# A two-layer decoder trunk on one Trainium2 core: the whole panels of the mixing sub-layers become split panels, and 14 of their low parts are formed by an adding DMA

## The reference

```python
h = modulate(x, 0)
x = x + 0.5 * gate(0) * swiglu(h, ffn_wg[l, 0], ffn_wu[l, 0], ffn_wd[l, 0])

h = modulate(x, 1)
z = h @ w_in[l]
q, k, v, u, gates = jnp.split(z, SPLITS, axis=-1)
q = apply_rope(...); k = apply_rope(...)
...  # 3 dilated windows x 4 heads, merged by a softmax over their denominators
y_attn = o.astype(x.dtype).reshape(b, s, ATTN_OUT_W) @ attn_wo[l]
y_conv = conv_module(u, conv_w[l], conv_b[l], conv_ln_g[l], conv_ln_b[l], conv_wo[l])
y = jax.nn.sigmoid(g_attn) * y_attn + jax.nn.sigmoid(g_conv) * y_conv
x = x + gate(1) * (y @ w_out[l])

h = modulate(x, 2)
x = x + 0.5 * gate(2) * swiglu(h, ffn_wg[l, 1], ffn_wu[l, 1], ffn_wd[l, 1])
```

## Time and profile before

| what | value |
|---|---|
| median of 3 runs | 1315.95 us (1315.18 to 1316.36) |
| the profiled execution | 1315.99 us, its span 1314.2 us |
| busy | PE 1260.4 us (96%), DVE 965.6 us (73%), ACT 546.3 us (42%), POOL 2.2 us |
| moved | 293.44 MB, mean 223 GB/s |
| mean granted clock of PE | 0.992 |

### The profile page before, as it was taken

One profiled execution on the slowest core, in us unless ns is written; L12 is line 12 of the kernel. 1 busy time (PEld: TensorE's weight loads), 2 busy tenths in 40 slices (PEclk: granted clock), 3 DMA queues, 4 the chain that ended last, 5 costly groups with the idle time before them and its releaser, 6 DMA issues.

```text
span 1314.2 us, 13852 instructions
## 1 busy us (share of the span) xinstructions
PE 1260.4 (96%) x5448; PEld 959.5 (73%) x5448; DVE 965.6 (73%) x1341; ACT 546.3 (42%) x576; POOL 2.2 (0%) x5
## 2 busy tenths in 40 slices
PE   3999999999998999999999999999999899999997
PEld 2588887765765777888878888876576677888885
DVE  5598886699996576877668887669999856644443
ACT  3343344432345355334354443353333453644331
POOL 0000000000000000000000000000000000000000
PEclk9999999999999999999999999999999999999999
DMA  9989994454323339889747889545532334454540
GB/s 378 413 304 373 362 368 168 160 180 157 128 97 128 139 121 370 339 330 353 286 178 271 334 332 349 184 169 184 176 128 97 128 131 176 175 192 176 195 173 33
DMA packets 52913, 293.44 MB, mean 223 GB/s; under 512 B 6640, under 2 KB 6896, under 8 KB 27120
## 3 DMA queue, kind: packets, MB, share of 16 engines
q1 hardware_dynamic: 51120, 289.38, 58.9%
q10 hardware_dynamic: 1728, 3.17, 0.7%
HBM read 291.45 MB, written 1.07 MB: 223 GB/s over the span
## 4 chain that ended last, share of the span: by engine, by line
PE 89%; DVE 4%; DMA 3%; ACT 2%; issue 2%; SPq 0%; DVEq 0%
PE ps L329 24%; PE ps L330 23%; PE ps L331 23%; PE ps L348 12%; DMA raw<-in_weights 2%; PE ps L515 1%; PE ps L396 1%; PE ps L537 1%; DMA ada_raw<-in_ada_w 1%; DVE hF L1084 1%; PE ps L485 0%; ACT L714 0%; PE ps L526 0%; DVE w_lo L997 0%; DVE hA_lo L997 0%
## 5 line engine op out<-in xcount | busy, mean ns | idle before, releaser
L997 DVE TENSOR_TENSOR w_lo<-raw,w_hi 128x2048 fp32r<-128x2048 f32 x176 | 401.2, 2287 | 38.7 <-ACT w_hi L708 38.7
L708 ACT CAST w_hi<-raw 128x2048 fp32r<-128x2048 f32 x176 | 334.2, 1908 | 171.6 <-PE ps L331 86.8
L329 PE MATMUL ps<-w_hi,hA_hi 128*128 128x512 f32 (+1 forms) x992 | 400.3, 404 | 5.5 <-DVE hA_lo L997 5.5
L331 PE MATMUL ps<-w_hi,hA_lo 128*128 128x512 f32 (+1 forms) x992 | 389.3, 392 | 0.0
L330 PE MATMUL ps<-w_lo,hA_hi 128*128 128x512 f32 (+1 forms) x992 | 389.2, 392 | 0.0
L329 PEld LDWEIGHTS ps<-w_hi,hA_hi 128*128 128x128 f32 x992 | 187.5, 189 | 53.7 <-issue 14.7
L331 PEld LDWEIGHTS ps<-w_hi,hA_lo 128*128 128x128 f32 x992 | 187.4, 189 | 42.9
L330 PEld LDWEIGHTS ps<-w_lo,hA_hi 128*128 128x128 f32 x992 | 187.6, 189 | 42.2 <-issue 2.9
L1186 DVE SCALAR_TENSOR_TENSOR work<-conv_in,par,work 128x256 f32<-128x256 f32 x480 | 193.8, 483 | 0.0
L1012 DVE SCALAR_TENSOR_TENSOR product<-ada_raw,c_bc 128x1024 f32<-128x1024 f32 x144 | 171.8, 1221 | 15.0 <-DMA ada_raw<-in_ada_w 14.6
L348 PE MATMUL ps<-raw,hF 128*128 128x512 f32 x384 | 171.4, 598 | 5.5 <-ACT hF L733 5.5
(11 more groups left out here) (121 smaller groups left out, 751.6 us busy)
## 6 DMA issues: line engine op xcount, KB each, us to landing
raw<-in_weights SPq DMA_DIRECT2D x200, 1024.0 KB, 4.8
ada_raw<-in_ada_w SPq DMA_DIRECT2D x144, 512.0 KB, 6.7
gate_bc<-gate_scratch ACTq DMA_DIRECT2D x6, 512.0 KB, 6.3
x<-in_x_tok SPq DMA_DIRECT2D x1, 1024.0 KB, 7.3
out_tok<-xn_h SPq DMA_DIRECT2D x4, 256.0 KB, 2.2
c_bc<-in_c_row SPq DMA_DIRECT2D x1, 512.0 KB, 4.4
c_bc<-in_g_row SPq DMA_DIRECT2D x1, 512.0 KB, 5.6
mask_all<-in_mask SPq DMA_DIRECT2D x1, 416.0 KB, 16.3
```

Of the source, the lines that this page charges most:

```text
L329: nc.tensor.matmul(out_ap, stat[0], mov[0], start=start, stop=False)
L331: return nc.tensor.matmul(out_ap, stat[1], mov[0], start=False, stop=stop)
L708: nc.scalar.copy(w_hi[:, s % HI, :], raw[:, p % RAW, :]).then_inc(hi_done, 1)
L997: return nc.vector.tensor_tensor(dst, whole, hi_part.bitcast(F32), ALU.subtract)
```

## The change

The list `WHOLE` goes; in the mixing parts every panel is split. Fourteen of the 34 (`ADDED`: the ten that were whole, and 10, 14, 21 and 26) get their low part in another way: right after the cast, ACT multiplies `w_hi` by -1 into `w_lo` (over the weights that the cast has just read), and POOL issues a DMA that reads the panel's 1 MB from HBM again and adds it to `w_lo` on the way. PE waits for the semaphore of that DMA in place of DVE's. For the other 20 DVE subtracts as before. The first 4 panels of the program stay whole. The counts of convolution steps, the number of slots and the order of PE's work stay.

```diff
-WHOLE = (5, 7, 9, 11, 13, 15, 18, 20, 22, 25)
-
 FIRST_WHOLE = 4
+
+ADDED = (5, 7, 9, 10, 11, 13, 14, 15, 18, 20, 21, 22, 25, 26)
...
 def is_whole(p):
-    return p < FIRST_WHOLE or p % LAYER_PANELS - FFN_PANELS in WHOLE
+    return p < FIRST_WHOLE
+
+
+def is_added(p):
+    return p % LAYER_PANELS - FFN_PANELS in ADDED
...
+            for i, p in enumerate(p for p in range(PANELS) if is_added(p)):
+                pool.wait_ge(minus_hi_done, i + 1)
+                pool.dma_start(w_lo[:, p % RAW, :], weights[p], accum_op=ALU.add).then_inc(lo_added[p % RAW], 16)
...
             def ready(p):
                 if is_whole(p):
                     pe.wait_ge(raw_in[p % RAW], 16 * (p // RAW + 1))
+                elif is_added(p):
+                    pe.wait_ge(lo_added[p % RAW], 16 * (adds(p) + 1))
                 else:
-                    pe.wait_ge(lo_done, splits(p) + 1)
+                    pe.wait_ge(lo_done, lows(p) + 1)
...
                 if s >= HI:
                     act_e.wait_ge(panel_done, SPLIT_PANELS[s - HI] + 1)
                 nc.scalar.copy(w_hi[:, s % HI, :], raw[:, p % RAW, :]).then_inc(hi_done, 1)
+                if is_added(p):
+                    act_e.wait_ge(hi_done, s + 1)
+                    nc.scalar.mul(w_lo[:, p % RAW, :], w_hi[:, s % HI, :].bitcast(F32), -1.0).then_inc(minus_hi_done, 1)
...
             def lo(p):
-                if p >= PANELS or is_whole(p):
+                if p >= PANELS or is_whole(p) or is_added(p):
                     return
```

More of the change, by code:

```diff
@@ L62, in splits, with lows, adds @@
     return sum(q < p for q in SPLIT_PANELS)
+def lows(p):
+    return sum(q < p and not is_added(q) for q in SPLIT_PANELS)
+def adds(p):
+    return sum(is_added(q) for q in range(p % RAW, p, RAW))
 def ffn_base(f):
@@ L226, in decoder_program @@
         hi_done, lo_done, panel_done = sem("hi_done"), sem("lo_done"), sem("panel_done")
+        minus_hi_done = sem("minus_hi_done")
+        lo_added = [sem(f"lo_added{i}") for i in range(RAW)]
         ada_step, bias_done, mods_done, gcol_done = sem("ada_step"), sem("bias_done"), sem("mods_done"), sem("gcol_done")
```

## The result

The changed kernel takes 1359.81 us (median of 4, 1358.88 to 1368.42) against 1316.15 us: ratio 1.0347, interval 1.0305 to 1.039. It is slower, as forecast, but by 43.7 us where 10.4 were forecast, and outside the range. The profiled execution took 1358.88 us, its span 1357.1 us, at a mean granted clock of 0.967 (0.992 before).

The account below looks back on a forecast made before the run. PE was taken to bound the kernel, 89% of the chain. 1316.0 + 1.6 (waits A to E against PE's gain, both layers) + 6.2 (clock) + 2.6 (adding DMA) = 1326.4 us; range 1315 to 1344.

Parts of the forecast that it names:

- the gain on PE: Mixing parts: ten panels a layer, split instead of whole, each save PE 1.28 us, 12.8 us a layer.
- A: pv(0), head 0: panel 21's minus pass stands ahead of the copies; PE waits 1.7 us a layer.
- E: pv(3), head 3: cast of 26 waits for panel 21, plus a minus; 4.9 us, 3.7 of it new.
- C: pv(1), head 1: copies stand behind the cast of 23, which waits for panel 18; PE waits 3.0 us.
- The clock: Waits over 2.5 us drop PE to the lower clock: four drops at 1.55 us, +6.2 us in all.
- D: p_turn(3), head 3: exponentials stand behind panel 25's cast, which waits for panel 20; PE waits 2.3 us.
- B: p_turn(1), head 1: exponentials stand behind panel 22's cast and minus; the cast waits for panel 17; 2.3 us.
- The adding DMA: At panel 5 the add may land late: between no wait and 2.7 us; 1.3 us a layer taken, +2.6.
- DVE: DVE loses four subtractions a layer and just keeps up, but for 0.6 us of PE waiting at the first rotary step.
- the adds jam the queue: Rival: eight adds and eleven loads between 248 and 315 us overfill the transfer engines; 1340 us, chance 0.22 (1334 and up).
- The clock holds: Rival: no clock drops and the add is hidden; 1317.6 us, no change that can be told; chance 0.13.
- The minus pass is cheap: Rival: minus passes at A, B, D and E cost nothing; 1311.9 us; chance 0.10 with any other gain.

Follow-up runs that it names:

- experiment 1: Changed kernel with ACT's casts and minus passes in the heads moved behind the copies or exponentials they stood ahead of; 1296.03 us, ratio 0.9843.
- experiment 4: Changed kernel with only the minus passes of panels 21, 22, 25 and 26 moved behind the copies or exponentials, casts left in place; 1328.44 us.
- experiment 3: Changed kernel with all 34 panels' low parts made by DVE, no minus pass and no adding DMA; 1341.06 us, ratio 1.0185.
- experiment 5: Kernel before the change with panel 21 cast twice ahead of head 0's copies; 1329.16 us, median of 10.
- experiment 2: Changed kernel without the adding DMA, PE taking minus the high part as low part of the 14 panels; 1346.28 us.

## Why the prediction was wrong

**Right: the gain on PE.** The whole panels are gone from the chain, and with the waits for ACT out of the way (experiment 1) the kernel is 20.3 us faster. Its profile still holds 8.0 us of waits for the add and the rotary step (5.8 + 2.2), which leaves 17.6 of the 25.6 us, and the 2.4 us of waits for the copies that the kernel before had are gone as well: 20.0.

**Right: the waits A to E.** Predicted 1.7, 2.3, 3.0, 2.3 and 4.9 us; in the first layer 1.7, 2.0 (1.69 and 0.34 at the two halves), 3.1, 2.1 and 5.0; in the second the same within 0.1, but for A with 2.45. Over both layers 26.4 us, net of the 2.4 of before, where 26.0 were forecast. Their reasons hold one by one: experiment 4 takes out the minus passes and leaves C and E at 3.1, experiment 3 has no minus pass at all and the same 3.1, experiment 1 takes out both.

**Wrong: "The clock".** This step failed. It counted drops behind C and E alone, with none behind waits of 2.3 us and less, at 1.55 us each: four drops, 6.2 us. The profile holds 33.5 us that no wait explains, 34.3 by the granted clock; fillers at three of the five places alone give back 23.6. Both halves were wrong. A wait of 1.7 us is enough: A has a spell in both layers, and in experiment 5 eight of ten executions are slow. D has one in both layers too. For B the zero held in the first layer and not in the second. And a drop is not always 3.2 us long: behind A and C it lasts some 10 us, so 5 us are lost, behind E some 7. I had taken both numbers from rows 8, the waits of 2.5 and 1.4 us, behind which PE does full split products at once; behind A, C and E it first does the small products of a head. Whether that is why those spells are longer no run shows: none varied it alone. A spell isn't set by the wait in front of it either: behind the same wait C of 3.1 us it is some 10 us in the changed kernel and longer in experiment 4 (0.54 from 355 to 370 us).

**Too small: "The adding DMA".** 1.3 us a layer were put at panel 5; the waits are 2.2 and 3.3 us, on either side of the upper bound (2.7). The profile gives the price of an add; its last row has the shortest, median and longest time to landing:

```profile
q1 hardware_dynamic: 51120, 289.38, 56.6%
q0 software_dynamic: 4032, 29.36, 11.1%
...
w_lo<-in_weights POOLq DMA_DIRECT2D x28, 1024.0 KB, 10.6
...
DMA to landing us min/median/max: 7.9/10.6/16.1
```

Per MB that is 0.111 x 1357.1 / 29.36 = 5.13 us of all engines against 2.65 for a load: 1.93 times, and 7.9 us to land at best, 10.6 in the median, against 4.9. Of the two ends the upper one was right. By the Trainium skill (Collectives: The Full Stack, The bandwidth ceiling: the fold count and why AG ≠ RS ≠ AR), which makes a reducing transfer of a collective half as fast for its two source reads, it would have been chosen; the trace agrees on the price, with 1.93. That the two reads are the reason no run here shows.

**Wrong in "DVE": 0.6 us at the first rotary step.** The waits are 2.4 and 0.6 us. I had looked only at DVE's own work. With the engines 0.99 busy, the load of panel 11 lands late, ACT waits 3.8 us for it, in order, and so gives DVE its next sigmoid late; DVE then has no idle time up to the rotary step:

```profile
280.00 0.69 DVE L1220 TENSOR_TENSOR glu<-sg,ps 128x512 f32<-128x512 f32 x1 [4.64 <-ACT sg L869]
```

Without the adds (experiment 2) the wait is gone. This is the rival "the adds jam the queue" in a mild form. Its cause was there (0.99), and the 13.5 us that the adds cost in all are not far from the 16.6 that its 1340 us held for them (2.6 and twice 7). But they are in other places: no add behind panel 5's is waited for, where the rival had those of 13 to 15 late.

**The rivals.** "The clock holds" is refuted by the rows of the granted clock. "The minus pass is cheap": it takes 1.92 us.

**The signs.** Of the three signs of being wrong one came true: the adds take over 10 us to land in the median. So did the wait of over 3 us at panel 5, in the second layer (3.3). PE was to be 5.8 us ahead at the scores of head 0 and is 2.3; it was to be some 6 us behind when pv(3) starts and is 20.1.

The sum with the measured terms: 1316.2 - 25.6 + 26.4 (A to E) + 8.6 (add, rotary step) = 1325.6; the clock adds the rest. That the kernel would be slower was forecast for reasons that held, but the gain and the waits A to E all but cancel, in the forecast as in the trace. The loss comes from the add, the rotary step and above all the clock, each of which was put too low.

## What to carry to other kernels

An engine that is less than half busy (here 47%) can still stop the one that bounds the kernel: ask of each new instruction what stands behind it in its engine's order. Ask of each ring of buffers how far ahead it lets work start: here the whole panels had skipped the ring, and with them gone its five slots reach less far. A wait of PE can cost more than its length: look at the granted clock behind it and at how long the same small products take there. Before a change with new waits is given up, move the helpers' new work behind what PE waits for: here the same instructions in another order were 63.8 us faster, and turned a loss of 3.5% into a gain of 1.6%.

## What the runs showed of the hardware

- A wait of PE of 1.7 us ahead of the small products of a head was followed by 10 us at the lower clock in the profiled execution of experiment 5; seven others of the ten are slow too (1324 to 1332 us, at a mean clock of 0.982 to 0.988), and two are not. The wait of 1.4 us in rows 7 and 8, ahead of full products, was followed by no drop. Whether a given wait lets the clock fall varies, between executions and between the two layers of one (B in the changed kernel), so that a kernel with one such wait a layer has times 15 us apart.
- Seven products that nothing reads, put into such a wait, kept the clock at 1.00, and the median went from 1329.2 to 1319.4 us.
- An adding DMA of 1 MB from HBM into SBUF took 1.93 times the transfer time of a load of that size here and landed in 7.9 us at best; POOL took 0.86 us to issue it.
